# Sliding mixer: scores of two query tiles issued together, and the probabilities' transposes ahead of the value product

## What is computed

```python
xn = rms_norm(h, norm_mix)
qa, ka, va, qb, kb, vb = split(xn @ w_in)
# sliding mixer: 16 chunks of 64 queries, band of 128 keys (this chunk and the one before)
sc = einsum('bcqhgd,bckhd->bchgqk', qc, kb) * HEAD_DIM ** -0.5
sc = where(valid, sc + bias, NEG_INF)
probs = softmax(concatenate([sc, sink], axis=-1), axis=-1)[..., :-1]
oa = einsum('bchgqk,bckhd->bcqhgd', probs, vb)
ob = differential_attention(qb, kb, vb, ...)      # dense mixer
h = h + concat(oa, ob) @ w_out
h = h + gated_conv_ffn(rms_norm(h), ...)
h = h + sigmoid(rms_norm(h) @ w_ple_gate) * (p @ w_ple)
out = rms_norm(h)
```

## Time and profile before

| | |
|---|---|
| time, median of 3 runs (lowest, highest) | 1230.24 us (1228.33, 1231.97) |
| span of the profiled execution | 1229.7 us |
| PE busy | 1197.1 us, 97% |
| DVE busy | 867.3 us, 71% |
| ACT busy | 517.8 us, 42% |
| sliding mixer in the trace | about 119 to 207 us |

### The profile page before, as it was taken

How to read it: one execution, slowest core, us unless ns; L and a number is a source line. 1 busy time by engine, 2 the same in 40 slices (tenths; PEclk the granted TensorE clock), 3 DMA queues, 4 the chain that set the end, 5 groups by cost and what they waited for, 6 DMA issues and landing times.

```text
span 1229.7 us, 17128 instructions
## 1 busy us (share of the span) xinstructions
PE 1197.1 (97%) x6167; PEld 1001.8 (81%) x6167; DVE 867.3 (71%) x1514; ACT 517.8 (42%) x1045; POOL 250.2 (20%) x291
## 2 busy tenths in 40 slices
PE   8999999999888999999999999999999999999997
PEld 7998887788676888888888888888888888888886
DVE  5433786877886577877787777877777999964443
ACT  4312665565655224433343343343344444733321
POOL 0000000344455122232332323323210000000000
PEclk9999999999899999999999999999999999999999
DMA  7464233111831512242322333233499533620101
GB/s 217 89 90 91 50 89 76 42 40 69 222 139 42 164 52 81 82 128 94 121 87 89 125 103 112 95 94 112 146 345 312 172 95 103 225 75 26 43 35 51
DMA packets 127916, 136.08 MB, mean 111 GB/s; under 512 B 15714, under 2 KB 93274, under 8 KB 127770
## 3 DMA queue, kind: packets, MB, share of 16 engines
q1 hardware_dynamic: 127834, 135.00, 36.1%
HBM read 96.77 MB, written 37.22 MB: 109 GB/s over the span
## 4 chain that ended last, share of the span: by engine, by line
PE 61%; issue 4%; DVE 2%; POOL 1%; ACT 1%; POOLq 0%; DVEq 0%; ACTq 0%
PE ps L1723 60%; PE ps L1729 1%; DVE xs L1474 1%; DVE h L1469 0%; DVE conv L1410 0%; POOL stat L687 0%; ACT xs L796 0%; DVE act_t L1185 0%; POOL stat L706 0%; POOL bias_a L712 0%; POOL more_f L714 0%; PE ps L2118 0%; ACT wbuf L793 0%; POOL o_t L709 0%; DVE h L1688 0%
## 5 line engine op out<-in xcount | busy, mean ns | idle before, releaser
L1723 PE MATMUL ps<-act_t,wbuf 128*128 128x512 f32 x1200 | 280.1, 389 | 0.5 <-DVE a_buf L1499 0.5
L1723 PEld LDWEIGHTS ps<-act_t,wbuf 128*128 128x128 f32 x1200 | 225.2, 188 | 47.5 <-DVE a_buf L1499 0.8
L1723 PE MATMUL ps<-wbuf 128*128 128x512 f32 x912 | 214.8, 390 | 0.0
L1723 PEld LDWEIGHTS ps<-wbuf 128*128 128x128 f32 x912 | 170.6, 188 | 35.1
L1723 PE MATMUL ps<-act_t,wq 128*128 128x512 f32 x624 | 152.2, 396 | 3.6 <-DVE wq L1187 3.0
L1723 PEld LDWEIGHTS ps<-act_t,wq 128*128 128x128 f32 x624 | 114.3, 188 | 30.8 <-issue 7.5
L687 POOL TENSOR_TENSOR stat<-stat 128x1 f32<-128x1 f32 x32 | 17.6, 549 | 420.9 <-DVE stat L1194 420.9
L793 ACT ACTIVATE wbuf<-raw 128x512 fp32r<-128x512 f32 (+1 forms) x107 | 69.0, 646 | 73.9 <-PE ps L1723 63.8
L1723 PE MATMUL ps<-hx,wbuf 128*128 128x512 f32 x408 | 95.7, 389 | 0.0
L1185 DVE TENSOR_TENSOR wbuf<-raw,wbuf 128x512 fp32r<-128x512 f32 (+1 forms) x107 | 87.4, 818 | 11.5 <-ACT wbuf L793 11.2
L1723 PEld LDWEIGHTS ps<-hx,wbuf 128*128 128x128 f32 x408 | 76.5, 188 | 15.9
(11 more groups left out here) (208 smaller groups left out, 1962.8 us busy)
## 6 DMA issues: line engine op xcount, KB each, us to landing
u_ops<-wbuf_f SPq DMA_DIRECT2D x77, 256.0 KB, 2.2
raw<-u_ops SPq DMA_DIRECT2D x77, 256.0 KB, 2.7
raw<-in_w_ffn_in SPq DMA_DIRECT2D x33, 512.0 KB, 3.8
g_ffn<-in_w_ffn_in SPq DMA_DIRECT2D x11, 512.0 KB, 3.9
act_f<-in_w_ffn_out SPq DMA_DIRECT2D x21, 256.0 KB, 4.3
w_raw<-in_w_in SPq DMA_DIRECT2D x10, 512.0 KB, 4.4
wbuf_f<-in_w_ffn_out SPq DMA_DIRECT2D x18, 256.0 KB, 5.9
x_in<-in_x SPq DMA_DIRECT2D x8, 512.0 KB, 3.8
```

What stands on the lines that cost most here:

```text
L1723: return nc.tensor.matmul(dst, lhs, rhs, start=start, stop=stop)
```

## The change

The twelve score matmuls go into a function `a_score(n)`. Before, each block issued its own; now every even block issues its own and then those of the next block, and odd blocks issue none. The even block waits for the logits of all blocks before it (`a_logits` at n instead of n - 1), because it overwrites the banks of both. In every block the transposes now stand ahead of the value product. ACT's, DVE's and SP's lists stay as they are.

```diff
+        def a_score(n):
+            s, t = n // NT, n % NT
+            if t == 0 and s == 1:
+                pe.wait_ge(S.unit_lo, 10)
+            for c in range(2):
+                ch = 2 * t + c
+                k0 = first_key(n, c)
+                for m, (a, b) in enumerate(SPLIT3):
+                    for g in range(2):
+                        rows = slice(HD * g, HD * g + HD)
+                        ins = mm(ps[:, 1 + 2 * (n % 2) + g, P * c + k0:P * (c + 1)],
+                                 q_a[rows, s, a, ch, :, :].rearrange("p u q -> p (u q)"),
+                                 k_a[rows, b, (ch - 1) * CHUNK + k0:(ch + 1) * CHUNK], m == 0, m == 2)
+            ins.then_inc(S.a_scores, 1)
+
         for n in range(NA + 3):
-            if n < NA:
-                s, t = n // NT, n % NT
+            if n < NA and n % 2 == 0:
                 if n >= 2:
-                    pe.wait_ge(S.a_logits, n - 1)
...
+                    pe.wait_ge(S.a_logits, n)
+                a_score(n)
+                a_score(n + 1)
+            if 2 <= n <= NA + 1:
+                m = n - 2
+                pe.wait_ge(S.a_probs, m + 1)
+                if m >= 1:
+                    pe.wait_ge(S.a_tlo, m)
+                for j in range(4):
+                    ins = nc.tensor.transpose(ps[:, 5, P * j:P * (j + 1)], e_a(m)[:, P * j:P * (j + 1)],
+                                              ident[:, :])
+                ins.then_inc(S.a_turned, 1)
             if n >= 3:
                 m = n - 3
                 pe.wait_ge(S.a_tlo, m + 1)
...
                 ins.then_inc(S.a_pv, 1)
-            if 2 <= n <= NA + 1:
-                m = n - 2
-                pe.wait_ge(S.a_probs, m + 1)
...
-                ins.then_inc(S.a_turned, 1)
             if NA <= n < NA + 2:
                 b_score(n - NA)
```

## The result

| | before | changed |
|---|---|---|
| median of 5 runs beside each other (lowest, highest), us | 1229.40 (1228.01, 1231.97) | 1233.16 (1231.72, 1233.70) |
| ratio of times, 95% interval | 1 | 1.0028 (1.0017 to 1.0039) |
| span of the profiled execution, us | 1229.7 | 1229.8 |
| sliding mixer in the trace: first scores to the first fill behind the last value product, us | 87.82 | 91.62 |

The changed kernel is slower by 0.28%, 3.4 us; no change (1.0) lies outside its interval. The two spans of the profiled executions say nothing of this: they differ by 0.1 us, though the stage that was changed takes 3.8 us more in the same two traces.

The account below looks back on a forecast made before the run. PE's own list was taken to bound the kernel (97% busy), with DVE close behind in the sliding mixer. Rounds +3.09, start +0.5 and block 16 +0.42 made +4.0 us on the median 1230.24: 1234.2 us, range 1229.5 to 1238.0.

Parts of the forecast that it names:

- forecast's own range: Total time 1232.0 to 1236.5 us, from uncertain value product turns and 0 to 0.8 us at the stage's start.
- Scores in pairs (1): PE's scores: two blocks' scores together take 1.47 us; PE's list gets 0.2 to 0.25 us shorter per two blocks.
- The wait for the copies (2): Odd blocks' transposes, straight behind the fill, wait 0.42 us for probabilities through ACT's copies and DVE; round 10.03 us.
- The split (3): In every second odd block a weight split keeps DVE busy, so the transposes are held 0.99 us; round 10.60 us.
- The rounds together (4): Blocks 4 to 15: six two-block rounds, three at +0.23 and three at +0.80 us, sum +3.09 us.
- The ends (5): Start of the stage +0.5 us, taken between 0 and 0.80; block 16 +0.42 us; block 17 covered.
- The stores (6): Landing of the value product's stores stays hidden (3.7 us); a 3.7 us landing would add 0.6 once or twice.
- All of it through to the end: The dense mixer hangs on the last fill, so the whole +4.0 us reaches the span: 1229.7 to 1233.7 us.
- The drain rival: Turns transposes to value product and value product to fill each cost 0.14 us: +2.9 us, 1237.1 us; chance 13%.
- The covered rival: Odd transposes not held, value product to transposes 2.90 us or less; only the shorter list remains: 1228.9 us; chance 12%.
- The clock rival: Granted clock drop in the dense mixer, 320 to 326 us, goes (1231.8 us) or another comes (1236.6 us); chance 13%.
- a fill over 0.8 after V: Sign in PE's timeline: a fill starting over 0.8 us after the value product means the drain is real.

Follow-up runs that it names:

- e6: Changed kernel with ACT's and DVE's copies and subtractions in the chain's order (transposes first) and the weight splits moved to later blocks; stage 86.31 us, ratio 0.9984.
- e3: Changed kernel with ACT copying the transposes before the value product's output and DVE normalising before subtracting for that output; stage 90.74 us, ratio 1.0024.
- e4: Changed kernel with weight splits moved: ACT's part to the next even block's end, DVE's to the next odd block behind the probabilities; stage 88.61 us, ratio 1.0001.
- e1: Changed kernel with the scores still in pairs but the value product put ahead of the transposes again, as before; stage 86.08 us, ratio 0.9985.
- e5: Scores in pairs and value product ahead of the transposes, as in e1, with the weight splits moved as in e4; stage 85.33 us, ratio 0.9978.

## Why the prediction was right, step by step

The forecast was +4.0 us and 1234.2 us, slower; measured +3.4 us by the ratio, +3.80 in the stage, 1233.16 us. Of the 1.04 us between 1234.2 and 1233.16, 0.84 is the base: the median of before was 1230.24 in three runs and 1229.40 in the five beside the changed kernel. The measured time lies under 1233.9, where the prediction had set the bound between no change and slower; that the kernel is slower rests on the interval of the ratio, which is narrower than the 0.3% assumed. The lower end of the forecast's own range, 1232.0, doesn't follow from the terms given for it: -0.5 at V to fill and -0.5 at the start make 1233.2.

- **Scores in pairs (1).** 1.49 for two, forecast 1.47. An unheld round, which e6 shows, takes 9.55 us, forecast 9.61.
- **The wait for the copies (2).** Forecast 0.42 and a clean round of 10.03; the round took 9.99. The chain from ACT's first copy was 2.91 again, to the hundredth. Against e6, where the odd transposes start 2.79 after their fill, they were held 3.17 - 2.79 = 0.38, which is all but 0.06 of what lies between 9.99 and 9.55. The term that was too large is the hand-over to PE: 0.06 (141.35 to 141.41), forecast 0.15. e3 and e6 show that it is this wait: with the two steps out of the chain it is gone.
- **The split (3).** The multiply ended 151.85 - (142.62 + 2.96) = 6.27 behind the fill, as forecast, and PE followed 0.06 later, not 0.15: a round of 10.50, forecast 10.60. e4 shows that it is the split.
- **The rounds together (4).** From the fill of block 3 to that of block 15, 194.65 - 132.63 = 62.02 us, against 59.00: +3.02, forecast +3.09. That it is so close is in part luck. The three clean rounds cost 0.19 to 0.22 (forecast 0.23) and two of the split ones 0.71 (forecast 0.80), but the one of block 11 cost 0.98, for the value product with 64 rows, which the sum didn't have; its 0.18 too much makes up for the two others.
- **The ends (5).** Fill of block 3 against the first scores: 132.63 - 117.17 = 15.46, before 134.81 - 119.76 = 15.05: +0.41, forecast +0.5. The number came out and its parts did not, and the 0.5 was a choice between 0 and 0.80: in e4, which takes the split away, this stretch is 131.31 - 117.31 = 14.00, so the new list saved 1.05 there and the wait behind the split cost 1.46. Block 16: 199.61 - 194.65 = 4.96 against 4.58: +0.38, forecast +0.42. Block 17: its transposes didn't wait, as forecast.
- **The stores (6).** In the changed kernel no copy of ACT waits for a store, as forecast. In e3 they did, when the store was issued later; this is where my expectation for e3 failed: I took two steps out of one chain and didn't ask what was queued behind the second.
- **All of it through to the end.** Counted from the first scores, the dense mixer began later by what the stage was longer, and the totals follow the stage in all eight kernels within their intervals. The prediction had named a stage that is longer with a span that is not as the sign of a wrong last step. The two spans show just that (1229.7 and 1229.8), but the 3.8 us went to the clock of that execution of before, as shown above.
- **The drain rival** falls by e6 and e1: 0.04 a round where it wanted 0.42. The value product does take 0.81 to the next fill instead of 0.72, but the transposes ahead of it take 0.41 instead of 0.46, and the fill behind it 2.90 instead of 2.93. Its sign, a fill over 0.8 after V, was set too near: 0.80 and 0.81 were measured, and the rounds show the 0.04. The drain that the Trainium skill states for a change of tiling mode (TensorEngine Tiling (Array Packing), Key Properties) shows here only into and out of the 64-row form: in the rows of before, 0.09 and 0.15, and in the changed kernel at the value products of blocks 3 and 11, 0.59 behind the transposes instead of 0.41. At those two the forecast's zero for T to V was wrong.
- **The covered rival** (not slower) falls: the wait, forecast 0.42 and measured 0.38, was there. It would have been the right one in e6, where the same order is faster than before.
- **The clock rival** was real in the single executions, 2.6 and 1.2 us in that of before, but not in the medians. The stretch that it named is in both: from 318 to 330 us the granted clock is 0.72 on average in either kernel.

## What to carry to other kernels

Before a consumer is moved ahead on the engine that bounds the kernel, lay the round trip of what it consumes (here 3.3 us, over two other engines' lists) against what is left of the engine's own work between the two (here a fill of 2.8 us instead of a whole round of 4.9). Moving it ahead has no use as long as the others' lists keep their old order, and here it had none with new lists either: e6, which has both cures, takes 86.31 us in the stage, e5 with the value product first 85.33. The shorter list that the pairs give was there all along: it pays by itself (e1), and more when the rare extra work on the answering engine is put into its idle time (e5).

## What the runs showed of the hardware beyond what I had expected

The granted clock differed between executions of the same code: in one profiled execution it was 0.57 on average from 26 to 30 us, in the other 1.00, with the same matmuls, and so 11 fewer of them done. Ahead of it PE had stood idle for 1.84 us in the one and for 0.73 in the other, for the same input tile. Effects of a few us in a kernel of 1230 us are therefore better read from the length of one stage in the trace, which repeated to 0.02 us between kernels that run the same rounds (87.82 and 87.84), than from spans.
